# Odd attention heads scored once with the queries on the partitions, and their probabilities turned by a DMA transpose

## The reference

```python
def one_chunk(args):
    ...
    s = jnp.einsum('bqhd,bkhd->bhqk', qb, kb).astype(jnp.float32) * scale + bias[None]
    s = jnp.where(valid[None, None, None, :], s, MASK_VALUE)
    p = jax.nn.softmax(s, axis=-1)
    return jnp.einsum('bhqk,bkhd->bqhd', p.astype(vb.dtype), vb)
```

## Time and profile before

| | us |
|---|---|
| median of 3 runs | 1652.11 |
| lowest and highest | 1651.89, 1652.51 |
| span of the profiled execution | 1648.8 |

### The profile page before, as it was taken

How to read it: one execution, slowest core, us unless ns; L and a number is a source line. 1 busy time by engine, 2 the same in 40 slices (tenths; PEclk the granted TensorE clock), 3 DMA queues, 4 the chain that set the end, 5 groups by cost and what they waited for, 6 DMA issues and landing times. The chain is left out here.

```text
span 1648.8 us, 44365 instructions
## 1 busy us (share of the span) xinstructions
PE 1609.6 (98%) x17944; PEld 1214.9 (74%) x17944; DVE 1063.1 (64%) x2200; ACT 838.7 (51%) x1589; POOL 666.8 (40%) x718
## 2 busy tenths in 40 slices
PE   7999999999999999999999999999999999999987
PEld 3455455468677777767777998889888898888964
DVE  7976866747565566557346666666666666666665
ACT  6654655522111111112136677776677677676785
POOL 2543433311101111111414555555555555555564
PEclk9999999999999999999999999999999999999999
DMA  7556556473614533552865443444334444344341
GB/s 249 211 192 218 201 206 221 167 280 124 228 64 169 201 128 106 179 192 87 224 222 147 145 124 110 136 140 139 116 118 136 143 136 119 114 138 136 98 142 52
DMA packets 144145, 258.01 MB, mean 156 GB/s; under 512 B 16040, under 2 KB 78008, under 8 KB 141896
## 3 DMA queue, kind: packets, MB, share of 16 engines
q1 hardware_dynamic: 142904, 253.88, 46.4%
q0 software_dynamic: 1040, 1.31, 0.5%
HBM read 151.40 MB, written 83.54 MB: 142 GB/s over the span
## 5 line engine op out<-in xcount | busy, mean ns | idle before, releaser
L2280 POOL TENSOR_TENSOR stages<-stages 128x512 f16<-128x512 f32 (+2 forms) x368 | 364.4, 993 | 350.6 <-ACT stages L2108 350.1
L1717 PE MATMUL bank<-middle,weights 128*128 128x128 f16 x1792 | 310.5, 219 | 1.2 <-DVE entry L1350 0.9
L1720 PE MATMUL bank<-middle,weights 128*128 128x128 f16 x1792 | 310.5, 219 | 0.0
L1719 PE MATMUL bank<-middle,weights 128*128 128x128 f16 x1792 | 310.4, 219 | 0.0
L2102 ACT ACTIVATE stages<-bank,log_ps 128x512 f32<-128x512 f32 (+2 forms) x368 | 221.9, 603 | 159.2 <-PE bank L1975 97.3
L1922 DVE CUSTOM_DVE_ANT_0 stages<-bank,stages 128x640 bf16<-128x640 f32 (+4 forms) x256 | 198.5, 776 | 73.8 <-PE bank L1887 73.5
L1119 PE MATMUL bank<-middle 128*128 128x256 f16 x784 | 213.7, 273 | 0.5 <-DVE stages L1259 0.5
L1122 PE MATMUL bank<-middle 128*128 128x256 f16 x784 | 213.7, 273 | 0.0
L1121 PE MATMUL bank<-middle 128*128 128x256 f16 x784 | 213.7, 273 | 0.0
L2108 ACT ACTIVATE stages<-stages 128x512 f16<-128x512 f32 (+2 forms) x368 | 202.8, 551 | 11.7
L1952 PE MATMUL bank<-entry,stages 128*128 128x512 f16 x768 | 190.8, 379 | 1.1 <-DVE stages L2164 1.1
(11 more groups left out here) (156 smaller groups left out, 3663.4 us busy)
## 6 DMA issues: line engine op xcount, KB each, us to landing
entry<-in_x SPq DMA_DIRECT2D x64, 512.0 KB, 3.7
h_ops<-middle SPq DMA_DIRECT2D x16, 1792.0 KB, 6.2
middle<-h_ops SPq DMA_DIRECT2D x112, 256.0 KB, 5.6
middle<-h_ops SPq DMA_DIRECT2D x49, 512.0 KB, 7.7
middle<-middle SPq DMA_DIRECT2D x384, 64.0 KB, 2.0
residual<-entry SPq DMA_DIRECT2D x32, 512.0 KB, 2.6
out<-entry SPq DMA_DIRECT2D x31, 512.0 KB, 2.6
entry<-residual SPq DMA_DIRECT2D x30, 512.0 KB, 5.1
```

What stands on the lines that cost most here:

```text
L1717: nc.tensor.matmul(dst, wh, hop3[:, o, 0, kt, :], start=(kt == 0 and s < 2 and pair == 0), stop=False, skip_group_check=True)
L1719: nc.tensor.matmul(dst, wh, hop3[:, o, 1, kt, :], start=False, stop=False, skip_group_check=True)
L1720: mm = nc.tensor.matmul(dst, wl, hop3[:, o, 0, kt, :], start=False, stop=(kt == 3), skip_group_check=True)
L2280: nc.gpsimd.tensor_tensor(p_l[:, h % 2, c + a:c + b], p32[g][:, a:b], p_h[:, h % 2, c + a:c + b], ALU.subtract).then_inc(A["pl_done"], 1)
```

## The change

Heads with an even number stay as they were, except that their probabilities have one buffer in place of two. A head with an odd number (`by_rows(h)`) goes another way:

- `maxima` multiplies both halves of the keys, so `wide` holds the full scores. `kl` of odd heads now holds the low halves on all 128 rows (one DMA more in `move_k`), and the mask and maximum rows of `qm` and `kl` are not needed for them (one DMA less in `move_q`).
- `maximum` adds the bias (`bias_r`, float32, all 640 columns), keeps the negated biased scores as float32 in `r32`, and takes their minimum; a small addition makes the shift `nm`.
- `row_exponential` (ScalarE) takes the exponential in place, with the row sum from its accumulator, and makes the high half in `r16`; `row_lo` (GpSimd) the low half.
- `turn` (SP) transposes all halves of the head from `r16` to `pT` by DMA, from tile 2 on in one DMA of 20 blocks of 128x128, in tiles 0 and 1 in four. `r16` and `pT` exist once.
- `row_values` (TensorE) multiplies `pT` by both halves of the values in 2 matmuls a block pair, of 128 and 64 columns; `attend` adds the two parts.
- Odd heads have no `max_rows`, `scores`, `add_bias`, `exponential` or `p_lo`.

For head (t, h), j = 0 is handled on ScalarE and GpSimd in head h - 2 and j = 1 in head h - 1.

```diff
+            def row_exponential(t, h, j):
+                at, side = row_count(t, h, j), h // 2 % 2
+                c = max(0, first_block(t) - j) * P
+                act.wait_ge(A["shift_done"], at + 1)
+                nc.scalar.activation(r32[:, j, c:640], r32[:, j, c:640], ACT.Exp, bias=nm[:, side, j:j + 1], scale=-1.0,
+                                     accum_out=psums[:, side, j:j + 1]).then_inc(A["rexp_done"], 1)
+                act.wait_ge(A["rexp_done"], at + 1)
+                at_least(act, turned, turns(HALF * t + h // 2))
+                nc.scalar.activation(r16[:, j, 0, c:640], r32[:, j, c:640], ACT.Copy).then_inc(A["rph_done"], 1)
...
+            def turn(t, h):
+                head = HEADS * t + h
+                sp.wait_ge(A["rpl_done"], row_count(t, h, 1) + 1)
+                at_least(sp, A["pv_mm"], head - 1)
+                if t >= 2:
+                    sp.dma_start_transpose(pT[:, :, :, :, :].rearrange("p j a i n -> p (j a i) n"),
+                                           r16[:, :, :, :].rearrange("p j a n -> p (j a n)")).then_inc(turned, 16)
+                    return
+                for j in range(2):
+                    skip = max(0, first_block(t) - j)
+                    for part in range(2):
+                        sp.dma_start_transpose(pT[:, j, part, skip:5, :], r16[:, j, part, skip * P:640]).then_inc(turned, 16)
...
+            def row_values(t, h):
+                pe.wait_ge(turned, turns(HALF * t + h // 2 + 1))
+                for j in range(2):
+                    blocks = [i for i in range(j, j + 5) if i >= first_block(t)]
+                    acc = pva[:, j * P:(j + 1) * P]
+                    for i in blocks:
+                        both = vr[:, ring(t, i), :].rearrange("p (a n) -> p a n", a=2)[:, :, h * (DH + 1):h * (DH + 1) + DH]
+                        nc.tensor.matmul(acc.rearrange("p (a n) -> p a n", a=2), pT[:, j, 0, i - j, :], both,
+                                         start=(i == blocks[0]), stop=False)
+                        mm = nc.tensor.matmul(acc[:, 0:DH], pT[:, j, 1, i - j, :], both[:, 0, :], start=False,
+                                              stop=(i == blocks[-1]))
+                mm.then_inc(A["pv_mm"], 1)
```

The order on TensorE and ScalarE, and SP's queue:

```diff
 PE           def head(t, h):
+                if by_rows(h):
+                    other(t, h, 0)
+                    if t2 < ATILES:
+                        maxima(pe, t2, h2, 0)
+                    if t1 < ATILES:
+                        max_rows(pe, t1, h1)
...
-                    if k is not None:
+                    if k is not None and not by_rows(h):
                         pe.wait_ge(A["exp_done"], seq(t, h, k) + 1)
                     values(*ahead(t, h, -1))
...
 ACT          def head(t, h):
-                exponential(t, h, 2)
-                exponential(t, h, 0)
-                other(t, h, 0)
-                if t1 < ATILES:
-                    max_row(t1, h1)
-                exponential(t, h, 1)
+                if by_rows(h):
+                    other(t, h, 0)
+                    if t1 < ATILES:
+                        max_row(t1, h1)
+                    if t2 < ATILES:
+                        row_exponential(t2, h2, 0)
+                else:
+                    row_exponential(t1, h1, 1)
+                    exponential(t, h, 2)
+                    exponential(t, h, 0)
+                    other(t, h, 0)
+                    exponential(t, h, 1)
...
 SP
                     load_v(sp, t, 1)
+                    turn(t, 1)
                     load_gate(sp, t, 1)
...
+                turn(t, 3)
                 move_k(sp, t + 1, 0)
                 move_q(sp, t + 1, 0)
+                turn(t, 5)
                 load_v(sp, t + 1, 0)
                 load_gate(sp, t + 1, 0)
                 if t > 0:
-                    for j in range(2):
-                        store(t - 1, j)
+                    store(t - 1, 0)
                 move_k(sp, t + 1, 1)
                 move_q(sp, t + 1, 1)
+                turn(t, 7)
+                if t > 0:
+                    store(t - 1, 1)
```

More of the change, by code:

```diff
@@ L146, in build @@
         Z = sb("stages", [P, 39168 // 4], F32)
+        X = sb("rows", [P, 11264 // 4], F32)
+        mx = sb("row_max", [P, 2, 2], F32)
+        nm = sb("row_shift", [P, 2, 2], F32)
+        psums = sb("row_sums", [P, 2, 2], F32)
+        pv32 = sb("row_values", [P, 2, DH], F32)
         wvg = view(R1, 0, (7, 2, 4, 512), F16)
@@ L1554, in build @@
         wob_loaded = [sem(f"a_wob_loaded{n}") for n in range(NKT)]
-        hop3_loaded = [sem(f"a_hop3_loaded{s}") for s in range(PRODUCTS)]
+        hop3_loaded = entry_loaded
+        turned = sem("a_turned")
         moved_k = [sem(f"a_moved_k{s}") for s in range(2)]
@@ L1600, in seq, with by_rows, row_count, turns @@
             if t == 0:
-                return h + k
-            return HEADS * 3 * t - 2 * HEADS + 3 * h + k
+                return h // 2 + k
+            return HALF * 3 * t - 2 * HALF + 3 * (h // 2) + k
+        def by_rows(h):
+            return h % 2 == 1
+        def row_count(t, h, j):
+            return HEADS * t + h - 1 + j
+        def turns(heads):
+            return 64 * min(heads, 2 * HALF) + 16 * max(heads - 2 * HALF, 0)
         def span(g, have):
@@ L1887, in maxima @@
                     mm = nc.tensor.matmul(wide[:, c:c + n * P], q, keys(ks, every, h, ring(t, i), n), start=True,
-                                          stop=True)
+                                          stop=not by_rows(h))
+                    if by_rows(h):
+                        mm = nc.tensor.matmul(wide[:, c:c + n * P], q, keys(kl, every, h, ring(t, i), n), start=False,
+                                              stop=True)
             mm.then_inc(A["max_mm"], 1)
@@ L2320, in a_phase_sp @@
                 if t == 0:
-                    for n in range(NKT):
-                        load_wob(n)
-                        for s in ((), (0, 1), (2, 3, 4), (5, 6))[n]:
-                            load_hop3(sp, 2, s)
+                    load_wob(0)
+                    load_wob(1)
+                    for s in (0, 1):
+                        load_hop3(sp, 2, s)
+                    turn(t, 1)
+                    load_wob(2)
+                    for s in (2, 3, 4):
+                        load_hop3(sp, 2, s)
+                    load_wob(3)
+                    for s in (5, 6):
+                        load_hop3(sp, 2, s)
                 else:
                     load_v(sp, t, 1)
+                    turn(t, 1)
                     load_gate(sp, t, 1)
```

193 lines of the change are left out of this document (121 added, 72 removed).

## The result

The change makes the kernel slower: the median of four runs is 1730.3 us (1727.2 to 1732.9) against 1652.0, a ratio of 1.047 (1.046 to 1.049). That lies inside the range given and on the forecast's side, but the forecast was +28 us and the change cost 78. The profiled run took 1727.2 us, 1.8 above its span of 1725.4.

A forecast was written before the change was run, and what follows sets the result against it. TensorE's own instructions, 98% busy, were taken as the bound. TensorE's gain of 43 us, tile-end stalls of 55 and edges of 14 summed to +26 us, a span of 1675 and some 1680 us measured; range 1614 to 1760.

The forecast's parts named there:

- TensorE's gain, 2.9 us a tile: TensorE, four odd heads a tile: 0.73 us less each, 43 us less over the kernel, a tile 48.7 us plus the stall.
- Mechanism and place of the stall: Head 7's turn waits behind 12 moves on SP, then ScalarE and TensorE wait: 3.9 us a tile, 55 us at 14 ends.
- The slope of 14 us for each us of T: At 14 tile ends, each us of the transpose's time from issue to landing beyond 2.4 us costs 14 us.
- T = 6.3: Transposing DMA of 640 KB, issue to landing: 6.3 us taken between 4.7 and 10, range 2.6 to 10.
- The price of 50 ns for a 256-byte piece: DMA engines in a turn: 50 ns a piece, 2560 pieces on 16 engines take 8 us, an upper bound of 10 us.
- The Trainium skill's estimate of 4.5: Turn's time from the page's 261 GB/s for a transposing DMA: 2.5 + 2.0 = 4.5 us, the sum then no change.
- The Trainium skill's 1309 ns a block: Page's time for one 128x128 block by DMA transpose; if blocks added up, 26 us for twenty, speaking against the change.
- The edges, 14 us: Tiles 0 and 1 and the last tile: slower turn loop, late turn and TensorE gain already idle, together 14 us more.
- All of it lies beside TensorE: Changed work on VectorE, ScalarE and GpSimd is covered by their 29 to 42% idle time; without cover 0.3 us a head.
- "T = 6.3 is hidden" for heads 1, 3, 5: Turns of heads 1, 3 and 5 have 8.2 us before TensorE needs their result, so 6.3 us causes no stall.
- budget of 8.2 us: Time for the turns of heads 1, 3 and 5: 6.27 + 5.88 + 4.1 - 3.0 - 5.0 us.
- Rival 1: The transpose is as quick as a plain copy, under 4.2 us: 1632 us, or 1614 at 2.4 or under; chance 0.37.

The follow-up runs named there:

- run 9: Second kernel of run 8 with the sum of an odd head's two value parts written back to PSUM: 1633.0 us, ratio 0.988.
- Run 1: Changed kernel with the last turn, turn(t, 7), issued ahead of the twelve moves on SP: 1682.3 us, ratio 1.019.
- run 4: Changed kernel with a plain DMA copy of the same 640 KB in place of the transpose from tile 2 on: 1703.9 us, ratio 1.032.
- run 5: Changed kernel with one transposing DMA a head in place of four in tiles 0 and 1: 1710.8 us, ratio 1.036.
- run 6: Changed kernel with the edits of Run 1 and run 5 together: 1655.9 us, ratio 1.003.
- run 8: Run 7 (first) and run 6 (second) with turn(t, 1) ahead of a values' load and three operand loads behind turn(t, 5): 1633.3 and 1647.0 us.
- run 2: Changed kernel with 27 unread matmuls ahead of TensorE's wait in head 0 of tiles 2 to 15: 1727.3 us, ratio 1.046.
- run 7: Run 6 with three 64-column products a block pair into the same columns, without VectorE's copy and addition: 1657.9 us, ratio 1.004.
- run 10: First kernel of run 8 with the shift's constant as an immediate instead of an SBUF tensor: 1635.7 us, ratio 0.991.

## Why the forecast had the sign and not the size

The forecast's +26 us of span split into +1.0 us a steady tile (3.9 stall, 2.9 gain), 12 us over the twelve tiles from 2 to 13, and 14 for the rest. Measured by the profiled spans, +76.6 us: +29.5 up to tile 2's second load of values, +37.3 (3.1 a tile) over the next twelve tiles, +9.8 from there to the end. So the steady tiles were short by 25 us and the edges by 25.

- **TensorE's gain, 2.9 us a tile: right.** It does not show in the time after, but run 9 reaches 48.7 us a tile over five tiles, which is the value worked out.
- **Mechanism and place of the stall: right.** The turn stands behind the moves, ScalarE's copy waits on it, TensorE on the exponential of group 2, once a tile. Run 1 takes it away (48 us). The slope of 14 us for each us of T is only argued, since run 4 changes more than T.
- **T = 6.3: too long.** It is 5.4. The price of 50 ns for a 256-byte piece, extrapolated from pieces of 1 and 2 KB, is 24 ns by the page's totals; 2560 pieces on 16 engines take 3.8 us, not 8. The stall is 3.1 us a tile, not 3.9, and this error, 10 us in twelve tiles, went the other way. The Trainium skill's estimate of 4.5 was too short; with it the kernel was to be unchanged. The Trainium skill's 1309 ns a block, summed, is far off: 20 blocks take 5.4 us, not 26. Nor is a turn as quick as a copy of the same bytes, as the Trainium skill's page "Advanced Engine Details and Errata", section "X-Bar Transpose (TRN2)", has it: 5.4 against 3.6 us.
- **The edges, 14 us: a step that failed, too small by 25** (39 measured). I had "four DMAs for a third of the data" as a T of 4.5, and did write that a larger SP cost per issue acts like a larger T, but priced an issue by the moves, 0.62 us. A transpose takes SP 1.1 us at least, four 5 to 6.5, in the tiles where a pair of heads has only 7.75. One DMA instead gives 19.5 us (run 5), and 26.4 where the last turn stands ahead of the moves already (run 6 against run 1). Even the first kernel of run 8 loses some 7 us at the edges. Its twelve steady tiles gain 25.5 us and its span only 18.5: by TensorE's first matmul of the output projection in tiles 2 and 14, the start is 1.7 us later (942.9 for 941.2) and the end 5.3 longer. What that is was not looked into.
- **"All of it lies beside TensorE": the other step that failed.** It put VectorE at nothing, and 2.9 us a steady tile, 35 us in twelve, were missing from the sum. I added up VectorE's small instructions and set them against its idle time of the whole stretch. Both of that was right and beside the point: what came was a longer duration of one instruction that is not new, because its input had moved from PSUM to SBUF, where GpSimd holds it up (618 for 280 ns). Run 9 prices it at 14 us with the other waits gone.
- **The rest of the 2.9 us a tile is not split by a run.** In the kernel after, TensorE idles 0.6 us a tile for VectorE and is busy for 51.0 us a tile instead of 48.7. The low clock accounts for at most 1.6 of these 2.3, yet with the clock kept up (run 2) the waits for VectorE grow, so that these two hide each other. From run 6 to run 9, VectorE's delay and the order of the loads together give 22.9 us.
- **"T = 6.3 is hidden" for heads 1, 3, 5: it held in the kernel that was forecast**, where TensorE waits 1.2 us in 400 behind the turn of head 5 and not behind that of head 3. But one T for all turns was too simple, though I had the rows of the operand loads at a DMA share of 0.96: in run 7 the turn of head 3 overruns its budget of 8.2 us four times in twelve. Moving the loads gives 9 us with VectorE's delay in place and 25 without it (run 8).

Together: 12 - 10 + 35 = 37 for the steady tiles and 14 + 25 = 39 for the edges, 76 for 76.6.

Rival 1, the other side, is out: T is 5.4 us and not below 4.2. But a kernel faster than before does not need a quicker transpose, only one that is issued in time and has nothing else in its way. The first kernel of run 8 turns in 5.6 us and is 1.1% faster than before.

## What to carry to other kernels

A DMA that somebody waits for is priced by its place in the issuing queue first (what stands ahead of it, and what the DMA engines are busy with when it gets there) and by its duration second; and a DMA split in four costs its queue four issues. When an operand moves from PSUM to SBUF, look at every VectorE instruction that now reads two tensors there while GpSimd runs, since its duration need not be that of the trace before. Two costs that hide each other show only when both are taken away, so an edit that brings nothing alone is worth a run on top of the other.

## What the runs showed of the hardware

- A transposing DMA of 20 blocks (640 KB in SBUF) lands after 5.4 us (4.8 to 7.3 in the kernel after; up to 9.0 behind seven loads in run 7); a copy of the same bytes after 3.6. SP is held for 3.4 us by the one and 0.5 by the other.
- A 256-byte packet of a turn took some 24 ns of a DMA engine, by the totals of the two kernels, against 67 for 1 KB by the earlier trace rows.
- A VectorE instruction with two SBUF inputs waited for GpSimd's to end: 64 columns took up to 1222 ns for 280 in the kernel after, one column 354 on average for 154 in run 10.
- A granted clock of 0.58 to 0.78 over 7 us at most tiles' starts, which looks alarming in the windows, was worth 3 to 10 us in 1730, with other delays beside it.
